# A third fixed expert, a sixth weight buffer, residual rows in DRAM, and the overflow rounds placed before the last expert tile

## The reference, cut to what matters

```
x = x + g1 * (concat(y_rwkv, y_conv) @ w_out)
h = rms_norm(x, norm2_g) * (1 + sc2) + sh2
g_idx = top1(softmax(h @ router_group_w + b))          # of 4 groups
e_idx = top2(softmax(logits of the 8 experts of the group))
for each of the two experts e of a token:
    out += weight * (silu(h @ gate[e]) * (h @ up[e])) @ down[e]   # 1024 x 256, 1024 x 256, 256 x 1024
x = x + g2 * out
y = rms_norm(x, final_norm_g)
```

## Time and profile before

| | |
|---|---|
| median of 3 runs | 1150.28 us (1144.94 to 1154.32) |
| profiled execution | 1150.49 us, span 1148.8 us |
| granted TensorE clock, mean | 0.846 of full |
| PE busy | 899.2 us, 78% |
| VectorE busy | 549.5 us, 48% |
| ScalarE busy | 299.9 us, 26% |
| output projection (about 681 to 779 us) | 98 us |
| routing (about 779 to 818 us) | 39 us |
| experts and overflow (818 to 1100 us) | 282 us |
| last scatters and the end (1100 to 1149 us) | 49 us |

### The profile page before, as it was taken

The page is one execution under the profiler, slowest core; times in us unless marked ns, Lnnn a source line. Parts: engine busy times, 40 slices in busy tenths (PEclk is TensorE's granted clock), DMA queues, the critical chain, the costliest instruction groups (busy, mean ns, idle before and its releaser), DMA issues.

```text
span 1148.8 us, 17262 instructions
## 1 busy us (share of the span) xinstructions
PE 899.2 (78%) x6827; PEld 544.8 (47%) x6827; DVE 549.5 (48%) x1108; ACT 299.9 (26%) x522; POOL 45.2 (4%) x50
## 2 busy tenths in 40 slices
PE   1599988999987797987958778972699984978754
PEld 0366544566665765767747434442334331324221
DVE  2426999855367767677542445357311110111016
ACT  2240000140655545465312341010011110101002
POOL 0000000000000000000000000000111201100010
PEclk9989998999988576755856978985699997989877
DMA  9843454111200202002062275113799999899342
GB/s 318 268 184 127 149 215 167 61 56 28 20 2 10 21 4 27 3 10 21 10 140 96 74 238 240 55 55 124 294 386 420 420 419 402 330 418 416 145 172 119
DMA packets 73870, 191.26 MB, mean 166 GB/s; under 512 B 42789, under 2 KB 45215, under 8 KB 59583
## 3 DMA queue, kind: packets, MB, share of 16 engines
q1 hardware_dynamic: 65536, 171.57, 41.7%
q0 software_dynamic: 5472, 10.53, 2.5%
q10 hardware_dynamic: 2783, 8.06, 1.9%
HBM read 179.83 MB, written 18.69 MB: 173 GB/s over the span
## 4 chain that ended last, share of the span: by engine, by line
PE 41%; DVE 17%; DMA 13%; ACT 8%; issue 4%; SPq 2%; DVEq 0%; POOLq 0%; ACTq 0%; POOL 0%
DMA arena<-in_expert_w_up 8%; PE bank L2134 8%; PE bank L539 5%; PE bank L1548 4%; DVE arena L969 4%; PE bank L2156 3%; ACT arena L845 2%; PE bank L1222 2%; PE bank L1209 2%; PE bank L1279 1%; PE bank L1308 1%; DMA arena<-winv 1%; PE bank L1282 1%; PE bank L1536 1%; DVE arena L1066 1%
## 5 line engine op out<-in xcount | busy, mean ns | idle before, releaser
L539 PE MATMUL bank<-arena 128*128 128x320 f32 x704 | 206.6, 448 | 2.1 <-ACT arena L389 2.1
L539 PEld LDWEIGHTS bank<-arena 128*128 128x128 f32 x704 | 134.5, 195 | 75.2 <-issue 26.5
L2134 PE MATMUL bank<-arena 128*64 128x512 f32 (+2 forms) x528 | 131.2, 654 | 32.0 <-DMA arena<-in_expert_w_up 31.1
L969 DVE SCALAR_TENSOR_TENSOR arena<-arena 128x655 f32<-128x655 f32 x116 | 104.7, 903 | 4.5
L2134 PEld LDWEIGHTS bank<-arena 128*64 128x64 f32 (+2 forms) x528 | 46.2, 150 | 115.3 <-issue 114.0
L2214 DVE TENSOR_TENSOR arena<-arena,bank 128x256 f32<-128x256 f32 x17 | 7.2, 422 | 158.8 <-ACT arena L2188 158.8
L1548 PE MATMUL bank<-arena 128*128 128x512 f32 x160 | 72.3, 610 | 0.0
L2156 PE MATMUL bank<-arena 128*64 128x512 f32 (+2 forms) x264 | 62.4, 599 | 10.3 <-DVE arena L2217 10.3
L1548 PEld LDWEIGHTS bank<-arena 128*128 128x128 f32 x160 | 30.9, 195 | 38.1 <-issue 38.1
L2188 ACT ACTIVATE arena<-bank 128x256 f32<-128x256 f32 x17 | 6.6, 386 | 140.5 <-PE bank L2134 140.4
L1308 PE MATMUL bank<-arena 64*64 64x64 f32 x320 | 31.8, 256 | 12.9 <-DVE arena L1136 12.9
(11 more groups left out here) (336 smaller groups left out, 1303.1 us busy)
## 6 DMA issues: line engine op xcount, KB each, us to landing
arena<-in_expert_w_gate SPq DMA_DIRECT2D x33, 1024.0 KB, 15.5
arena<-in_expert_w_up SPq DMA_DIRECT2D x33, 1024.0 KB, 19.1
arena<-in_expert_w_down SPq DMA_DIRECT2D x33, 1024.0 KB, 19.1
arena<-in_ada_w SPq DMA_DIRECT2D x12, 2048.0 KB, 8.6
arena<-in_w_in SPq DMA_DIRECT2D x22, 512.0 KB, 3.9
arena<-expert_rows SPq DMA_DIRECT2D x10, 512.0 KB, 7.5
arena<-in_x_sample SPq DMA_DIRECT2D x8, 512.0 KB, 6.0
arena<-in_w_out SPq DMA_DIRECT2D x1, 4096.0 KB, 16.4
```

The source lines that it names most:

```text
L539: mm = nc.tensor.matmul(psum[4 + 2 * (n % 2) + half][:, 0:HALF], wring[:, n % NWIN, k], hT[:, k, half * HALF:(half + 1) * HALF], start=(k ...
L969: chain(nc.vector.scalar_tensor_tensor(acc, src, w, acc, ALU.mult, ALU.add))
L2134: mm = nc.tensor.matmul(psum[2 + n % 2][r, :], xeT[:, n % 2, c, r], gu[:, :, c, :], start=(c == 0), stop=(c == KD - 1))
```

## The change

- `FIXED_EXPERTS` is now (0, 8, 16), so three experts are loaded before routing. The fixed pair tile has experts 8 and 16; expert 0 shares a pair tile with rank 11.
- The 17 tiles are in the order: fixed pair, P P S Q P H H Q P S S S S Q P P. The first P is the one with expert 0.
- The last P tile (`NSTAT` is 16) is taken out of the pipelined loop and done after the overflow rounds, in the same manner as a round: nothing of it ahead. Its two weight loads stand behind the overflow round's load on SyncE's queue (`turn_of`).
- A sixth weight buffer (`NB = 6`). It covers the place where `x2` and `sh2b` lie, so `x2` is stored to DRAM (`x2d`) by ScalarE's queue in each round, right behind `h2`, and read back (`x2e`) when the 16 tiles are done, with `g2b` and the final gain. `s_h2st` now counts two stores for each tile.
- The fixed loads wait until the first `sq_pos` has landed (`s_pos2`), and the load of `sh2b` is later. With `NB = 6` all loads but the first four still wait for the overflow list, now counted on `s_ids`.
- The ranking has two more small VectorE operations for the rows and two for the lanes.
- Of the scatters, those of tiles 14 and 15 are issued after the overflow round's, that of the last tile at the end.

```diff
-SECOND, COLD, FIXED = NHOT + NPAIR, NHOT + 2 * NPAIR, NEXP - 2
-FIXED_EXPERTS = (0, 16)
+SECOND, COLD, FIXED = NHOT + NPAIR, NHOT + 2 * NPAIR - 1, NEXP - 3
+FIXED_EXPERTS = (0, 8, 16)
-ROWS = [(NTILE - 1, (FIXED, FIXED + 1))]
+ROWS = [(NTILE - 1, (FIXED + 1, FIXED + 2))]
-for _kind in "SQHPPPPSQSPPSSQ":
+for _kind in "PPSQPHQPSSSSQPP":
...
-        NB = 5
+        NB = 6
...
+            for c in (1, 0):
+                sp.dma_start(gain2[:, c], modrows[c:c + 1, 4 * D:5 * D].broadcast_to([P, D])).then_inc(s_modb, 16)
+            sp.wait_ge(s_mixa, 1)
             sp.dma_start(x2[:, 4], tok_src(4)).then_inc(s_x2in, 16)
...
+            for c in (1, 0):
+                sp.dma_start(sh2b[:, c], modrows[c:c + 1, 3 * D:4 * D].broadcast_to([P, D])).then_inc(s_modb, 16)
...
-            for c in range(2):
-                sp.dma_start(g2b[:, c], modrows[c:c + 1, 5 * D:6 * D].broadcast_to([P, D])).then_inc(s_fg, 16)
+        def turn_of(i):
+            return i if i < NEXP - len(ROWS[NTILE - 1][1]) else i + 1
...
                 act.dma_start(h2d[i * P:(i + 1) * P, :], h2).then_inc(s_h2st, 16)
+                act.dma_start(x2d[i * P:(i + 1) * P, :], x2[:, i]).then_inc(s_h2st, 16)
...
-                chain(nc.vector.tensor_scalar(own, src, float(FIXED_EXPERTS[1]), 2.0, ALU.is_equal, ALU.mult))
-                chain(nc.vector.scalar_tensor_tensor(own, src, float(FIXED_EXPERTS[0]), own, ALU.is_equal, ALU.add))
+                chain(nc.vector.tensor_scalar(own, src, float(FIXED_EXPERTS[2]), 3.0, ALU.is_equal, ALU.mult))
+                for e in (FIXED_EXPERTS[0], FIXED_EXPERTS[1], FIXED_EXPERTS[1]):
+                    chain(nc.vector.scalar_tensor_tensor(own, src, float(e), own, ALU.is_equal, ALU.add))
...
+        NSTAT = NTILE - 1
+        NLOAD = NEXP - len(ROWS[NSTAT][1])
...
                         "o (p c) f -> p (o c f)", p=P)).then_inc(s_edw[OVB] if j == 2 else s_egu[OVB], 16)
-            sp.wait_ge(s_escat[0], rounds * 16 + 16 * (OV_SCATTERS + 1))
-            sp.wait_ge(s_escat[1], 16 * (NTILE // 2))
+            for n in range(NLOAD, NEXP):
+                experts_load(n)
+            sp.wait_ge(s_edown, NSTAT)
+            sp.dma_start(x2e, x2d.rearrange("(i p) d -> p i d", p=P)).then_inc(s_fg, 16)
+            for c in range(2):
+                sp.dma_start(g2b[:, c], modrows[c:c + 1, 5 * D:6 * D].broadcast_to([P, D])).then_inc(s_fg, 16)
+            sp.dma_start(fgain, ins["final_norm_g"].rearrange("(o n) -> o n", o=1).broadcast_to([P, D])
+                         ).then_inc(s_fg, 16)
...
-            scatter(pool, NTILE - 2)
-            scatter(pool, NTILE - 1)
+            scatter(pool, NSTAT - 2)
+            scatter(pool, NSTAT - 1)
+            pool.wait_ge(s_eoa, rounds + (NSTAT + 1))
+            pool.wait_ge(s_eod, rounds + (NSTAT + 1))
+            pool.sem_inc(s_ovgo, 1)
+            pool.indirect_dma_start(out=yexp, out_offset=At(ap=tab[:, ROWS[NSTAT][0], 1:2].bitcast(U32), axis=0),
+                                    in_=eo[:, 0], in_offset=None,
+                                    bounds_check=last_row, oob_is_err=False).then_inc(s_escat[0], 16)
...
             turn(0)
-            for n in range(NTILE):
+            for n in range(NSTAT):
                 gate_up(n)
-                if n + 1 < NTILE:
+                if n + 1 < NSTAT:
                     turn(n + 1)
                 down(n)
...
             sp_out()
-            for n in range(2):
+            sp.wait_ge(s_pos2, 16)
+            for n in range(len(FIXED_EXPERTS)):
                 experts_load(n)
             sp.wait_ge(s_ids, 1)
-            sp.wait_ge(s_h2st, 16 * TILES)
-            for n in range(2, 4):
-                experts_load(n)
-            sp.dma_start(fgain, ins["final_norm_g"].rearrange("(o n) -> o n", o=1).broadcast_to([P, D])
-                         ).then_inc(s_fg, 16)
-            sp.wait_ge(s_ovst, 1)
-            for n in range(4, NEXP):
+            sp.wait_ge(s_h2st, 32 * TILES)
+            experts_load(len(FIXED_EXPERTS))
+            sp.wait_ge(s_ids, 2)
+            for n in range(len(FIXED_EXPERTS) + 1, NLOAD):
                 experts_load(n)
```

More of the change, by code:

```diff
@@ L1361, in build @@
         late = regp.take(NCONST - NKEEP)
-        regs = Region(ebuf[NB - 1], ebuf[1])
+        assert regp.at <= ebuf[NB - 1]
+        x2, sh2b = regp.take(TILES, D), regp.take(2, D)
+        regs = Region(low, ebuf[2])
         conv = regs.take(4, CT)
@@ L1366, in build @@
         ROUTING = 7 * CT + D
-        regs.at = ebuf[NB - 1] + ROUTING
+        regs.at = low + ROUTING - 2 * D
+        xtmp, xsq = regs.take(D), regs.take(D)
         rega = Region(wbase, unit_at)
@@ L2070, in pe_overflow @@
                 mm.then_inc(s_edown, OVSTEP)
+            pe.wait_ge(s_gat[NSTAT % NG], 16 * (NSTAT // NG + 1))
+            pe.wait_ge(s_eTa, rounds + NSTAT)
+            pe.wait_ge(s_eTd, rounds + NSTAT)
+            for c in range(KD):
+                mm = nc.tensor.transpose(psum[c // 4][:, (c % 4) * P:(c % 4 + 1) * P], xe[:, NSTAT % NG, c::KD], ident)
+            mm.then_inc(s_et, 1)
+            pe.wait_ge(s_eTa, rounds + (NSTAT + 1))
+            pe.wait_ge(s_eTd, rounds + (NSTAT + 1))
@@ new lines, in pe_overflow @@
+            for k in ROWS[NSTAT][1]:
+                n = turn_of(LOADS.index(k))
+                pe.wait_ge(s_egu[n % NB], EGU_FROM[n % NB] + 32 * (n // NB + 1))
+            for c in range(KD):
+                for r, b in column_tiles(NSTAT):
+                    gu, _ = wview(b)
+                    mm = nc.tensor.matmul(psum[2 + LASTP][r, :], xeT[:, LASTP, c, r], gu[:, :, c, :],
+                                          start=(c == 0), stop=(c == KD - 1))
+            mm.then_inc(s_gu, 1)
@@ new lines, in pe_overflow @@
+            pe.wait_ge(s_hid, rounds + (NSTAT + 1))
+            pe.wait_ge(s_hT, rounds + NSTAT)
+            for c in range(2):
+                mm = nc.tensor.transpose(psum[4][:, c * P:(c + 1) * P], hid[:, LASTP, c::2], ident)
+            mm.then_inc(s_ht, 1)
+            pe.wait_ge(s_hT, rounds + (NSTAT + 1))
+            pe.wait_ge(s_eoa, rounds + NSTAT)
+            pe.wait_ge(s_eod, rounds + NSTAT)
+            for k in ROWS[NSTAT][1]:
+                n = turn_of(LOADS.index(k))
+                pe.wait_ge(s_edw[n % NB], 16 * (n // NB + 1))
@@ L2072, in act_overflow @@
+            for h in range(2):
+                for c in range(2):
+                    for r, b in column_tiles(NSTAT):
+                        _, wd = wview(b)
+                        mm = nc.tensor.matmul(psum[5 + h][r, :], hidT[:, LASTP, c, r], wd[:, c, h * 512:(h + 1) * 512],
+                                              start=(c == 0), stop=(c == 1))
+            mm.then_inc(s_edown, 1)
         def act_overflow():
             act = nc.scalar
-            with act.Fori(0, overflow_rounds(act)) as i:
-                act.wait_ge(s_et, i * OVSTEP + (NTILE + OVSTEP))
-                act.wait_ge(s_gu, i + NTILE)
+            rounds = overflow_rounds(act)
@@ L2273, in act_end @@
                 act.wait_ge(s_xf, i + 1)
[L2274 removed]
+                chain.announce(nc.scalar.activation(fsq, x2e[:, i], ACT.Square, accum_out=small[:, i:i + 1]),
                              s_xstat, 2 * TILES + i + 1)
```

148 lines of the change are left out of this document (87 added, 61 removed).

## The result

The changed kernel takes 1140.05 us (median of 13 runs, 1135.54 to 1143.83), the one before 1150.28 (13 runs beside them, 1144.94 to 1154.79). The profiled execution took 1140.05 us with a span of 1138.3, 10.4 less than that of before.

The account below looks back on a forecast made before the run. DMA of weights was taken to bound the experts' stage, the tensor engine the output projection. 0.8 + 1.8 - 6.5 - 2.6 = -6.5 us from 1150.49 gives 1144; 8-in-10 range 1131 to 1152.

Parts of the forecast that it names:

- The projection's loss: Output projection: round 0's break goes, but round 1's position rows land late beside the fixed loads; 1.8 us lost.
- the worst bound: Output projection: 4 us lost if round 1's position rows land only when the fixed loads are done.
- The rival in which the rows are in time: Output projection: round 1's position rows land by about 711, 8.3 us gained, 1134 in all; chance 0.28.
- The gaps: Experts' stage: sixth buffer and new order close three gaps in the DMA stream, 8.3 us gained.
- the start of tile 15: Experts' stage, pair tile before the overflow round: its gate_up starts at about 1043, from 1039.4 to 1047.
- The tail: From tile 15's gate_up through overflow round and last tile: 50.4 us, down ends at 1093.4, 6.5 us gained.
- The slow tail: Rival: the tail's three gate_up run at half clock, 15.7 us more, 1159.7; chance 0.10.
- The weights of the last tile: Tail: they land at latest at 1069 and are wanted at 1079, so they are no limit.
- Scatters: End of the experts' stage: one scatter left at the end in place of three, 2.6 us gained.
- Ranking: Chain from the counts to the table: four more VectorE operations, 0.8 us lost.
- Reading back: End of kernel: x2e, g2b and the gain, 10 us of DMA, hidden with 27 us of cover; no cost.
- The second rival: Experts' stage: the DMA gaps move elsewhere, tile 15 starts at 1050, only scatters gained, 1150; chance 0.18.

Follow-up runs that it names:

- e1: Changed kernel with the nine fixed loads issued only when all four position rows have landed; 1132.61 us, ratio 0.9839 to the kernel before.
- e2: Changed kernel with the store of x2 put behind the load of the next round's position rows on ScalarE's queue; 1136.53 us, ratio 0.9885 to the kernel before.
- e3: Changed kernel with each load of position rows issued as soon as x2 of the round before is done; 1131.96 us, ratio 0.9827 to the kernel before.
- e6: Changed kernel with the weights in rotation through five of the six buffers; 1152.31 us, ratio 1.0006 to the kernel before.
- e7: Changed kernel with the tiles in nearly the old order, six buffers kept; 1146.79 us, ratio 0.9948 to the kernel before.
- e5: Changed kernel with all 17 tiles in the pipelined loop and the overflow round behind them; 1151.6 us, ratio 0.9994 to the kernel before.
- e8: Changed kernel with the third fixed expert loaded only when the rank list is ready; 1135.81 us, ratio 0.9849 to the kernel before.
- e10: e3 with a fifth load issued ahead of the overflow list, into the buffer of x2 and sh2b; 1126.83 us, ratio 0.9784 to the kernel before.
- after: The changed kernel itself, in its one profiled execution; 1140.05 us, the kernel's ratio to the one before 0.9899.
- e9: Changed kernel with nearly the old order of tiles and five buffers in rotation; 1151.28 us, ratio 0.9998 to the kernel before.

## Why the prediction was right

The sign, the parts and their places held, but no term of the sum came out at its size, and that the sum is within 4 us is in part luck: tile 15 came later than forecast and the tail behind it ran shorter. Forecast less measured, by the profiles, the errors are 2.0 us too little lost in the projection and 3.3 too much gained up to tile 15, against 7.1 too little gained in the tail, 0.8 in the scatters and 0.8 in the ranking.

- *The projection's loss.* Forecast 1.8 us, measured 3.8 from the start of the sums, at the turn of round 2 (67.9 us for 64.1) as at that of round 4. The turns were forecast at 702, 725 and 747 and came at 701.5, 726.9 and 748.8. The rows landed at 718, not 716.3: the queue got 112 GB/s over 14 us where I had taken 145 from a sample of 2 us. The last two fixed matrices land at 716.6 and 719.5, so it came out at the worst bound that I had named (4 us, rows that land only when the fixed loads are done) and not at the rate of the sample. The mechanism is shown by e1, e2 and e3, each of which takes away one part of it. The rival in which the rows are in time is what e3 makes of it.
- *The gaps.* Those of the earlier trace rows went away, but the 8.3 us taken from their shares came as 5.6: the second matrix of load 26 lands 226.8 us behind the first load of the list in place of 232.4. It takes the sixth buffer (e6) and the new order with it (e7's share is 0.96 from 947 to 1000). The step that failed is the one from the share of the gaps straight to the start of tile 15, on both sides of it. The load came at 1049.4, not at 1042.5 + 2.6, since it landed while the share was already falling. And the tensor engine, which I had ready at some 1037 to 1041, was ready only at 1047.9, since tile 14 had itself waited for weights until 1032.84; a load in time would have gained 1.75 us and no more. I had also said that a buffer is free before the stream reaches it, for each kind of tile: that of the overflow round's load isn't, SyncE waits 18.8 us for it, and the share is not near 1 up to 1060 but only up to 1032. And I had read the gap of 982 to 1000 wrongly: SyncE issued 13 matrices in it, so it had something to send. Of the three gaps only that of 960 to 982 is one in which it sent nothing (no issue from 958.33 to 981.84); in that of 830 to 847 it sent 8.
- *The tail.* Forecast 50.4 us from tile 15 to the end of `down`, measured 43.3. I had taken each `gate_up` from rows at partly low clock, 9.22 and 8.71; all three ran at 7.1, which is 5.4 of the 7.1 us. Another 1.4 is the last tile, which stands 0.83 us for its turned rows where I had copied the 2.09 of the overflow round, and turns them in less time. The slow tail was the wrong side to be afraid of, but it isn't absent: tile 15 to rows back is 47.6 to 51.9 us in these profiles (without e5), with a `gate_up` now of 7.1 and now of 8.7 for the same break of 2.07 us. So part of the 7.1 is the one execution that was profiled. The weights of the last tile were no limit, as said (e5 shows the price of having them as the limit).
- *Scatters.* 2.6 forecast, 3.4 measured.
- *Ranking.* 0.8 forecast. The list of ranks now comes 0.8 us later behind the turn of round 4 (798.34 - 775.85 = 22.5 against 794.13 - 772.48 = 21.7). But from the issue of the first gather to the first turn of expert rows it is 3.4 us in place of 4.2, and that hid it for the tensor engine: 45.1 us in both. I had not seen that. It isn't that fewer weights are on their way beside the gather: e8 and e10 have six matrices there, as many as before, and show 3.6 and 3.5. The cause stays open.
- *Reading back* cost nothing: the last of it landed at 1085.0, and was wanted behind 1102.

The second rival, that the gaps stay, is refuted by the windows of after; e6 and e7 show where they come back. The change as written is three things that pay more together than by themselves: the place of the overflow round (11 us by e5), the sixth buffer and the order (12 and 6 by e6 and e7, 11 together by e9), less what the later and larger fixed loads cost the projection. Without the overflow round's place or without the sixth buffer the whole gain is gone, without the new order half of it is left. The third fixed expert pays nothing anywhere (e8).

## What to carry to other kernels

Before moving a bulk transfer, look at what small transfer of another queue it will run beside: 0.5 MB took 14.8 us behind two stores and beside nine weight loads, and issuing it 10 us earlier in its own queue was worth 8 us, nearly as much again as the whole change brought. A deeper buffer and an order of work made for it should be tried together: with the overflow round in its new place, the order alone showed nothing (e6 against e9), the buffer alone 5.8 us (e7 against e9), both 11.4. Take each part of such a change out by itself at the end: the third fixed expert was a part that only cost. When a stage is bound by DMA, look for idle time in front of it and ask which of its loads already has its address and its buffer.

## What the runs showed of the hardware that I had not expected

When SyncE's queue has nothing behind its last loads, the DMA engines do not finish together. In the windows of after, the share falls from 1.02 over 0.86 and 0.57 to 0.25 between 1032 and 1049, and the matrices already issued land all the same only at 1049.4 and 1051.9. In the kernel before, the overflow's load did this too: share 0.77 from 1069 to 1072 and 0.28 from 1072 to 1077, landing at 1077.0. So the last load before a pause lands later than its bytes at 420 GB/s would say. The packed trace has each packet and each of the 16 completions of a matrix, and they show why. From 1028 to 1032 there are 16 or 17 packets in flight at any time; at 1045, 1046, 1047 and 1048 there are four. The 16 completions of the matrix issued at 1028.07 are spread from 1033.2 to 1051.9, the last four of them behind 1048.9. So some of the 16 engines run dry early and about four have work left. Why these are behind, and whether the gathers and scatters load them more, wasn't tried and stays open.

The other is that the same short break costs the clock in one execution and not in the next: `gate_up` of the overflow round behind 2.07 us took 7.11 us in after and in e8, 8.75 in e6, 8.74 in e1. Over all twelve profiles, with breaks of 2.07 to 2.10 us, it is 8.7 to 8.8 in four and 7.1 in eight. These are executions of different kernels, one each; after and e1 have the same code in this stage. The Trainium skill ("TensorE: Matmul & The Clock Gate", section "What's actually happening") says that the phase of the monitor runs free of the kernel, so that the transition shifts from run to run. The rows agree in that the same form at the same break has two durations, but no run here shows the phase itself; a forecast should carry both, here 1.6 us for each such break.
